# Stores of the inverse spectra: from GpSimd's DMA queue to ScalarE's, with another order of the rows

## The reference

```python
def hyena_mixer(u, w_in, b_in, conv_w, conv_b, ..., skip, w_out, b_out):
    L = u.shape[1]                                   # 1024
    z = short_conv(u @ w_in + b_in, conv_w, conv_b)
    x0, x1, v = jnp.split(z, 3, axis=-1)
    s = (v * x1).astype(jnp.float32)
    g = hyena_filter(L, ...)                         # 2048 x 1024
    n = 2 * L
    y = jnp.fft.irfft(jnp.fft.rfft(s, n=n, axis=1) * jnp.fft.rfft(g, n=n, axis=0)[None],
                      n=n, axis=1)[:, :L]
    y = (y + s * skip.astype(jnp.float32)).astype(u.dtype) * x0
    return y @ w_out + b_out
```

## Time and profile before

| | us |
|---|---|
| median of 3 runs | 2445.98 |
| lowest, highest | 2445.57, 2446.84 |
| the profiled execution, its own time | 2445.98 |
| its span (first to last instruction) | 2444.2 |
| TensorE busy | 2360.0 (97%) |
| VectorE, ScalarE, GpSimd busy | 1107.9, 604.0, 657.8 |
| mean granted clock of TensorE | 0.986 |

### The profile page before, as it was taken

The page is one execution under the profiler, slowest core; times in us unless marked ns, Lnnn a source line. Parts: engine busy times, 40 slices in busy tenths (PEclk is TensorE's granted clock), DMA queues, the critical chain, the costliest instruction groups (busy, mean ns, idle before and its releaser), DMA issues.

```text
span 2444.2 us, 29269 instructions
## 1 busy us (share of the span) xinstructions
PE 2360.0 (97%) x11692; PEld 1899.7 (78%) x11692; DVE 1107.9 (45%) x1131; ACT 604.0 (25%) x672; POOL 657.8 (27%) x378
## 2 busy tenths in 40 slices
PE   7999999799999999999997999999999999999996
PEld 5666773478888888888886888889897877778885
DVE  6765445542662165413366837263543124500533
ACT  4333324422100001002123636262622011111011
POOL 2212211122333333323241121222222233323331
PEclk9999999999999999999998999999999999999998
DMA  4133239512221223112111212020214221112231
GB/s 155 51 122 123 85 134 369 187 43 78 95 86 52 77 80 109 43 43 70 51 61 35 104 36 69 26 77 26 77 34 181 94 78 56 56 43 69 95 121 69
DMA packets 77507, 211.51 MB, mean 87 GB/s; under 512 B 24182, under 2 KB 28088, under 8 KB 77178
## 3 DMA queue, kind: packets, MB, share of 16 engines
q1 hardware_dynamic: 64794, 172.72, 20.7%
q10 hardware_dynamic: 8288, 29.36, 3.1%
q0 software_dynamic: 4352, 8.40, 1.1%
HBM read 165.36 MB, written 40.37 MB: 84 GB/s over the span
## 4 chain that ended last, share of the span: by engine, by line
PE 75%; DVE 3%; ACT 1%; issue 0%; ACTq 0%; DVEq 0%
PE ps L1209 63%; PE ps L539 5%; DVE T L1857 1%; PE ps L1483 1%; PE ps L586 1%; PE ps L605 1%; PE ps L568 1%; PE ps L606 1%; PE ps L607 1%; PE ps L1231 0%; DVE XN L1887 0%; PE ps L1240 0%; DVE X L2181 0%; DVE H L1880 0%; PE ps L505 0%; PE ps L524 0%
## 5 line engine op out<-in xcount | busy, mean ns | idle before, releaser
L1209 PE MATMUL ps<-H,whi 128*128 128x512 f32 x4000 | 1082.3, 392 | 21.9 <-DVE H L1924 11.3
L1209 PEld LDWEIGHTS ps<-H,whi 128*128 128x128 f32 x4000 | 749.9, 188 | 198.5 <-issue 29.6
L1209 PE MATMUL ps<-H,wlo 128*128 128x512 f32 x2000 | 617.7, 390 | 0.0
L1156 POOL CAST whi<-wraw 128x1024 fp32r<-128x1024 f32 x174 | 182.5, 1049 | 1573.0 <-PE ps L1209 844.9
L1158 POOL TENSOR_TENSOR wlo<-wraw,whi 128x1024 fp32r<-128x1024 f32 x178 | 453.6, 2548 | 53.4 <-ACT whi L673 39.5
L1209 PEld LDWEIGHTS ps<-H,wlo 128*128 128x128 f32 x2000 | 376.5, 188 | 79.3
L1209 PE MATMUL ps<-A,whi 128*128 128x512 f32 x1472 | 397.8, 392 | 8.2 <-DVE A L2213 4.9
L1209 PEld LDWEIGHTS ps<-A,whi 128*128 128x128 f32 x1472 | 278.0, 189 | 68.0 <-issue 5.3
L1209 PE MATMUL ps<-A,wlo 128*128 128x512 f32 x736 | 228.1, 391 | 0.0
L1209 PEld LDWEIGHTS ps<-A,wlo 128*128 128x128 f32 x736 | 139.3, 189 | 29.3
L2097 DVE TENSOR_TENSOR T<-ps,T 128x1024 f32<-128x1024 f32 x22 | 26.9, 1224 | 155.7 <-PE ps L1209 155.7
(11 more groups left out here) (337 smaller groups left out, 2310.6 us busy)
## 6 DMA issues: line engine op xcount, KB each, us to landing
wraw<-in_panels SPq DMA_DIRECT2D x181, 512.0 KB, 3.6
mw<-in_modp SPq DMA_DIRECT2D x24, 512.0 KB, 3.5
g<-gsp SPq DMA_DIRECT2D x16, 512.0 KB, 3.7
gr<-g SPq DMA_DIRECT2D x16, 512.0 KB, 9.8
bs<-s SPq DMA_DIRECT2D x16, 512.0 KB, 9.4
YB<-yi POOLq DMA_DIRECT2D x16, 512.0 KB, 8.8
X<-in_xT SPq DMA_DIRECT2D x4, 1024.0 KB, 10.8
s<-sa SPq DMA_DIRECT2D x8, 512.0 KB, 2.7
```

Of the source, the lines that this page charges most:

```text
L1156: nc.gpsimd.tensor_copy(whi[:, s, :, :], wraw[:, s, :, :]).then_inc(hi_made, 1)
L1209: last = mm(p[:, c * step:(c + 1) * step], w[:, ws, k, :], operand(act, a, k, c * step, step), start=(q == 0 and w is whi and a == 0), sto ...
```

## The change

The store is issued by ScalarE, directly behind its copy to `yi` and a wait for that copy, and no longer by GpSimd. `y_rows` places groups 0 to 3 in partitions 0 to 31, 4 to 7 in 32 to 63 and so on, each still with a step of 4, and the rows of `idft` are loaded in the order that fits. The semaphores of the stores are now those of three early loads, which `kf` shared before, and `kf` gets three of its own.

```diff
-        kf_in = [(x_in[1 + u], 16) for u in range(3)] + [(g1_out[u], 16 * (N2 // 2 + N2 // 4)) for u in range(2)]
+        kf_in = [(sem(f"kf_in{u}"), 0) for u in range(3)] + [(g1_out[u], 16 * (N2 // 2 + N2 // 4)) for u in range(2)]
...
-        y_out = [sem(f"y_out{u}") for u in range(3)]
+        y_out = x_in[1:4]
...
-            return y_out[g % 3], 16 * (g // 3 + 1)
+            return y_out[g % 3], 16 + 16 * (g // 3 + 1)
...
         def y_rows(g):
-            b = 64 * (g % 2) + 32 * (g // 8) + g // 2 % 4
-            return slice(b, b + 29, 4)
+            return slice(g % 4 + 32 * (g // 4), g % 4 + 32 * (g // 4) + 29, 4)
...
-            rows = d["cst"][:, CST["idft"]:CST["idft"] + HALF].rearrange("(w b s r) c -> s w r b c", w=2, b=4, s=2)
-            for q in range(4):
-                sp.dma_start(cst[32 * q:32 * q + 32, CST["idft"]:CST["idft"] + HALF], rows[q // 2, q % 2, :, :, :]
+            for a in range(0, P, 32):
+                sp.dma_start(cst[a:a + 32, CST["idft"]:CST["idft"] + HALF],
+                             d["cst"][a:a + 32, CST["idft"]:CST["idft"] + HALF].rearrange("(b r) c -> r b c", r=8)
                              ).then_inc(const_in, 16)
...
-            for g in range(GROUPS):
-                pool.wait_ge(spec_ev, g + 1)
-                pool.dma_start(YB[y_rows(g), :, :], yi[g % 3][:, :]).then_inc(y_stored(g)[0], 16)
...
                 A_(yi[g % 3][:, :], ps[Y_SLOT][:, :], ACT.Copy).then_inc(spec_ev, 1)
+                act.wait_ge(spec_ev, g + 1)
+                act.dma_start(YB[y_rows(g), :, :], yi[g % 3][:, :]).then_inc(y_stored(g)[0], 16)
```

## The result

The changed kernel takes 2460.74 us (median of 4 runs, 2460.12 to 2461.47), the kernel before beside it 2445.78 us (2444.3 to 2446.84). The ratio is 1.0063, with a 95% interval of 1.0051 to 1.0076: 15.0 us slower. Its profiled execution has a span of 2458.2 us, 14.0 more than that of before.

What follows compares the result with a forecast made beforehand. The prediction took the spectral loop to be bound by DMA, with TensorE 9% behind. To 2445.98 us it added +15.5 for the crowded half and -3.0 for the wait behind the loop, giving 2458.5 us, range 2443 to 2473.

Steps and rivals of the forecast that it cites:

- What bounds the loop: Spectral loop, 371 to 445 us: bound by DMA at 4.71 us a group, with TensorE 9% behind at 4.29.
- Semaphores, idft, GpSimd's and ScalarE's instructions at 0: Semaphore changes, idft loads, issues leaving GpSimd, and ScalarE's added wait and issue (gq copy 0.7 to 1.1 us later): 0.
- Rival 3: ScalarE becomes the bound in the loop, its issues stretched to 2.8 us; alone +10 to +20 us; chance 0.05.
- The crowded half, +15.5: Spectral loop: stores on eight engines crowd one half, 6.06 us a group against 4.71; 11.5 x 1.35 = +15.5 us.
- rival 1: Stores stay spread and the hardware queue is simply quicker: 2442.2 us, with the clock 2439.8; chance 0.15.
- The wait behind the loop, -3.0: Last copy's end to TensorE on YB: 8.5 us falls to 5.5, packets 2.55 to 3.0 plus 1.3 fixed; bounds 4.5, 8.5.
- The clock, 0: First 48 inverse matmuls behind the loop: low clock costs 2.4 us, change taken as 0, bounds -2.4 and +2.
- rival 4: TensorE's clock falls to half within the loop, 8.6 us a group, +30 more: 2490 us; chance 0.03.
- The sum: Whole kernel: +15.5 in the loop and -3.0 behind it, +12.5 us; forecast 2458.5 us.
- the signs: If right: 136 packets a store, about 6 us a group, share 0.75 to 0.85, last copy near 460, wait under 6.5.
- rival 2: Loop crowding half-hidden by SP's ring of three groups and a lagging yi: 2449 to 2451 us; chance 0.12.

Runs made afterwards that it cites:

- e9: The kernel before, with the loads of gr and bs cut to a quarter of the columns from group 3 on: 2445.38 us, 0.9988.
- e10: The changed kernel, with the loads of gr and bs cut to a quarter of the columns from group 3 on: 2445.96 us, 0.9993.
- e5: The kernel before, where ScalarE also waits for each copy to yi and issues a small DMA to scratch memory: 2447.89 us, 0.9995.
- m1: Separate program with transfers only, no arithmetic; 12-group stages vary the store's queue and half. With loads: ScalarE 68.3 (one half), 72.8 (two); GpSimd 75.7, 69.2 us.
- e1: The changed kernel with the old order of the rows, even and odd groups in alternating halves, stores still from ScalarE: 2465.77 us, 1.0074.
- e3: The kernel before, with one small 8-row DMA issued by GpSimd behind each store: 2448.87 us, 0.9998.
- e2: The kernel before with only the new order of the rows, stores still from GpSimd's queue: 2460.50 us, 1.0054.
- e8: The changed kernel, each store writing 16 partitions of 32 KB in one half for eight groups in a row: 2456.17 us, 1.0029.
- e12: The changed kernel, each store writing 16 partitions of 32 KB in one half, the halves taking turns: 2456.75 us, 1.0041.

## Why the prediction was right, and where it wasn't

**What bounds the loop.** Right. DMA does, with TensorE close behind: light loads take the whole difference away (`e9`, `e10`).

**Semaphores, idft, GpSimd's and ScalarE's instructions at 0.** Right. The issue took 0.62 us, the gq copy started 0.76 us behind the yi copy in most groups, and `e10`, with the full issues and light loads, stands at 0.9993 (0.9983 to 1.0003); `e5` has the wait and a shorter issue, 0.9995. Rival 3 is out.

**The crowded half, +15.5.** Measured: +12.3, the delay of the last copy, made of other factors than mine. A group took 6.46 us from group 6 to 12 where 6.06 was forecast. The same sum with the durations of after gives loads 48.3 x 1.278 MB / 16 = 3.86 and store 41.4 x 0.524 MB / 8 = 2.71, together 6.57. By this reading the store's term was sized right (2.85), and the loads' 3.21, which I had left as it was before, was 0.65 too small. It is a reading: it takes the loads' packets to be as dear on the crowded eight as on the others, and the trace doesn't name a packet's engine. The count was off the other way: 11.5 groups at the dearer pace were forecast, but up to group 6 the prefetch covered them. The delay is -0.6 at group 6, 6 x 1.76 = 10.6 up to group 12, and 2.35 from there to the last copy (22.00 against 19.65 us), all but 0.1 of it between groups 12 and 13 (6.59 against 4.30 us). The forecast's size in this term owes something to two errors of opposite sign.

The reason I gave was half right. Eight engines a store, and the same eight each time, which no row of before had shown, are shown now: by the 136 packets, by the loads that land in two halves 8.6 us apart, and by the share of 0.46 in `m1`. That the one half adds to it on ScalarE's queue: not shown, `e1` is no quicker than the changed kernel with its halves in turn. The Trainium skill, "DMA: Bandwidth & Descriptors", section "Why a DMA increments its semaphore by 16 and not by 1", has a hardware-queue DMA use the lowest-numbered engines; by that rule `e1` and the changed kernel should be alike. Their loads' landings are (8.2 and 8.6 us between the two parts), and 2465.77 and 2460.74 us, with ratios whose intervals overlap, agree. Its rotating cursor for GpSimd's queue was not borne out by `e3`, nor refuted. The halves' rule of the Trainium skill, "SBUF — State Buffer", section "Door 1: The DMA port swizzle", fits `e2` (12.6 us for one half on GpSimd's queue) but not `e8` against `e12`: on sixteen engines, one half or turns of halves give 1.0029 and 1.0041. The advice of the Trainium skill's "SBUF — State Buffer" that rival 1 leans on is given for a DMA beside VectorE work that keeps GpSimd from writing the DMA's descriptors; no run here shows such a stall.

What stays open is why packets get dearer (in the changed kernel half of the loads' 4 KB packets still take 0.16 us, as nine of ten did before, and the slowest tenth 0.24 and more): from 40 to about 50 engine-us per MB for the loads in every variant that touches the queue or the rows under full loads, on sixteen engines and on eight, with halves in turn or not. In the changed kernel's 6.57 us this is 0.65, and the store on eight engines 1.20 (2.71 against 1.51). In `e12` the store is spread, yet loads (0.77) and stores (0.39) are so much dearer that the sum is 5.88 us a group, measured 6.06. Between kernels with their rows in the same halves, sixteen engines and partitions instead of eight give back 8 us, in turns (1.0074 to 1.0041) as in one half (1.0063 to 1.0029), 3.2 and 3.8 of them behind the loop; 7 to 10 us of loss remain. None of the variants shows what slows a packet, whether it is which engine meets which partitions, what it reads, or something else; I can't say.

**The wait behind the loop, -3.0.** Wrong: 8.6 us from the end of the last copy (458.22) to 466.80, as before (8.5). The step that failed is the landing of "2.55 to 3.0" for packets behind a fixed 1.3. The landing that I took it from was of a store on sixteen engines. Stores on one set of eight also queue behind each other: stores 13, 14 and 15, issued at 450.87, 455.16 and 458.25, have their last increments at 457.03, 461.83 and 466.56. The DMA queues of the changed kernel from 450 to 460 us, with hardly anything but stores, read

```profile
q10 hardware_dynamic: 343, 1.33, 47.0%
```

which is 75.2 engine-us for 2.54 stores, 29.6 a store and 3.7 us on each of eight. When store 14 has landed, SyncE's queue goes on with the panel loads that wait for it (461.85), beside store 15. Why a store takes 4.7 to 4.8 us behind another one here, when it took 2.9 to 3.0 us in `m1`, wasn't found. In `e10`, with light loads, the wait from the end of the last copy is 8.7 us. The upper bound, 8.5 and no gain, is what came.

**The clock, 0.** The first 48 inverse matmuls took 6.98 us where they had taken 8.23, 1.25 less and within the bounds. But inside the loop the granted clock fell once, to a mean of 0.55 from 433 to 440, with the signal matmuls of group 12 at 3.69 us instead of 1.95; from 426 to 433 TensorE had been busy 4.14 us. So rival 4 came in small. These 16 matmuls are 1.74 us longer, but the loop would have waited anyway: the load of `bs` for group 13 had its last increment at 441.75, and its signal matmuls start at 441.79. Behind the loop the low clock lies in other places than before, and this is what the rest of the span is made of. The delay falls from 12.4 to 9.6 us by 508 us: the 1.25 is part of that, and the clock of before was also 0.50 from 490.9 to 497.7, where now it is 1.00. Then it grows again; the kernel before and, behind it, the changed one:

```profile
1347.13 1.99 PE L505 MATMUL ps<-LRT,wup_h 16*128 16x512 f32 x8 [1.50 <-ACT LRT L1751]
...
1352.36 1.07 PE L1209 MATMUL ps<-H,whi 128*128 128x512 f32 x4
```
```profile
1356.87 3.21 PE L504 MATMUL ps<-LRT,wup_h 16*128 16x512 f32 x8 [1.50 <-ACT LRT L1749]
...
1365.32 1.07 PE L1205 MATMUL ps<-H,whi 128*128 128x512 f32 x4
```

The delay is 9.7 us at the first row of each and 13.0 at the last: the clock is 0.50 from 1357.5 to 1364.3 in the changed kernel and 1.00 over the same work before. A last 0.9 us comes in the same way at the end, at 2427. What moves these stretches isn't shown; the light kernel before, `e9`, has the one near 1350 as well.

**The sum.** +15.5 - 3.0 = +12.5 was forecast; +12.3 in the loop, 0.1 behind it and 1.6 later in the span came, and 15.0 between the medians. The loop came out 3.2 below its term, the wait 3.1 above, so the sum was met better than its terms: the number owes that to luck. The last 1.6 us are the net of the clock's stretches, about -2.8, +3.2 and +0.9, and of 0.2 more.

**Signs and rivals.** Of the signs, 136 packets and the period came; the share fell only to 0.92 up to 436 us where 0.75 to 0.85 was forecast, TensorE's longer waits name `bs` alone, ScalarE has none for YB<-yi, the last copy starts at 457.20 instead of near 460, and the first inverse matmul comes 8.6 us behind its end instead of under 6.5. Rival 1 fell with the period. Of rival 2 a part is true, the six groups that the prefetch covers, but not its total. None of the kernels with full loads beat the one before.

## What to carry to other kernels

Where the DMA share is 1.00 a store's queue and its rows are part of the loop's price, though its bytes stay the same: count the packets of one DMA in the profile to see how many engines serve it, and take the load per engine, not the mean. If the increments of the neighbours' semaphores come in two groups, some engines are behind. Price the neighbours of the moved transfer too, by engine-us per MB in each queue's row; here the loads, which nobody touched, make 0.65 of the 1.86 us by which a group is dearer in the sum. And a landing is to be taken from a transfer with the same number of engines and the same queue of others before it.

## What the runs showed of the hardware that I had not expected

- All stores to eight partitions from ScalarE's queue ran on one set of eight engines, whichever half they wrote (DMA share 0.46 and 0.47 in `m1` with three in flight), and beside full loads each load's second half of increments came 8.6 us after the first.
- The order of the partitions alone, 16 stores of 8 rows from the same queue, is worth 12.6 us in a loop of 75 us, with every engine busy in both cases (share 1.00 and 1.04, 382 and 308 GB/s).
- The last store, to eight partitions, lands no sooner from ScalarE's queue than from GpSimd's: 8.4 and 8.2 us after the issue; one to sixteen partitions takes 4.8, from ScalarE's queue.
- Stores alone took 2.75 to 3.04 us for 512 KB in `m1` whatever queue and half they used (33.0 to 36.5 us for 12, at 173 to 191 GB/s), half the 370 GB/s of the loads alone.
